# A two-block network on one core: the gate table of the expert layer built by indirect accumulating DMAs instead of one-hot products

## The reference

```python
q = (xt @ wq).reshape(T, 8, 2, 128)
s1, s2 = q[:, :, 0] @ k1.T, q[:, :, 1] @ k2.T            # (T, 8, 128) each
v1, i1 = top_k(s1, 16); v2, i2 = top_k(s2, 16)           # first choice, per half
cand = v1[..., :, None] + v2[..., None, :]               # 256 pair sums per head
sc, pos = top_k(cand, 16)                                # second choice
eidx = (i1 * 128 + i2 at pos); gate = softmax(sc)        # (T, 128) each
act = gelu(sum_d xb[t, d] * u_tab[eidx[t, k], d])
out[t] = sum_k gate[t, k] * act[t, k] * v_tab[eidx[t, k]]
```

## Time and profile before

| what | value |
|---|---|
| median of three runs | 3072.06 us |
| span of the profiled execution (the page gives no other time of it) | 3070.2 us |
| PE busy | 3026.7 us (99%) |
| DVE / ACT / POOL busy | 2206.3 / 1491.0 / 418.5 us |
| granted TensorE clock | 0.996 over the span |
| chain that ended last | PE 85%, DVE 5%, POOL 4%, issue 4% |
| DMA | 579.55 MB, 189 GB/s mean |

### The profile page before, as it was taken

One profiled execution on the slowest core, in us unless ns is written; L12 is line 12 of the kernel. 1 busy time (PEld: TensorE's weight loads), 2 busy tenths in 40 slices (PEclk: granted clock), 3 DMA queues, 4 the chain that ended last, 5 costly groups with the idle time before them and its releaser, 6 DMA issues.

```text
span 3070.2 us, 56622 instructions
## 1 busy us (share of the span) xinstructions
PE 3026.7 (99%) x19590; PEld 2701.3 (88%) x19590; DVE 2206.3 (72%) x3890; ACT 1491.0 (49%) x2330; POOL 418.5 (14%) x246
## 2 busy tenths in 40 slices
PE   8999999999999999999999999999999999999998
PEld 7889888888888888899999988888899999988887
DVE  6677566666756667669788777776659978767776
ACT  4455444444644444444455445555444454545554
POOL 0001000000011002038700000001118810000000
PEclk9999999999999999999999999999999999999999
DMA  6543255555434554457766677775447765577775
GB/s 222 187 160 119 90 169 188 168 187 187 136 98 129 187 190 135 166 183 228 217 189 182 203 241 241 240 241 181 161 158 226 227 196 183 181 247 242 240 240 187
DMA packets 213022, 579.55 MB, mean 189 GB/s; under 512 B 23744, under 2 KB 88544, under 8 KB 212368
## 3 DMA queue, kind: packets, MB, share of 16 engines
q1 hardware_dynamic: 209504, 563.67, 57.2%
q0 software_dynamic: 3376, 13.94, 1.4%
HBM read 541.34 MB, written 36.18 MB: 188 GB/s over the span
## 4 chain that ended last, share of the span: by engine, by line
PE 85%; DVE 5%; POOL 4%; issue 4%; ACT 2%; DMA 1%; SPq 0%; POOLq 0%; ACTq 0%; DVEq 0%
PE acc L745 32%; PE work L688 24%; PE work L698 9%; PE work L700 5%; POOL wsp L661 3%; PE acc L1142 3%; PE acc L807 3%; PE acc L1276 3%; DVE wsp L438 1%; ACT wsp L435 1%; PE work L1176 1%; PE work L944 1%; PE work L958 1%; PE work L1064 0%; POOL st L563 0%
## 5 line engine op out<-in xcount | busy, mean ns | idle before, releaser
L438 DVE TENSOR_TENSOR wsp<-ring,wsp 128x1024 fp32r<-128x1024 f32 x824 | 1004.4, 1227 | 489.9 <-ACT wsp L435 489.0
L435 ACT ACTIVATE wsp<-ring 128x1024 fp32r<-128x1024 f32 x944 | 984.6, 1052 | 577.4 <-PE work L688 373.8
L688 PE MATMUL work<-xsp,wsp 128*128 128x256 f32 x7872 | 982.3, 285 | 3.2 <-DVE xsp L1762 2.0
L688 PEld LDWEIGHTS work<-xsp,wsp 128*128 128x128 f32 x7872 | 955.1, 192 | 6.3 <-issue 3.0
L745 PE MATMUL acc<-wsp,hsp 128*128 128x512 f32 x4128 | 955.9, 390 | 4.7 <-DVE hsp L1850 1.9
L745 PEld LDWEIGHTS acc<-wsp,hsp 128*128 128x128 f32 x4128 | 769.5, 188 | 168.6 <-issue 4.3
L698 PE MATMUL work<-xsp,wsp 128*128 128x512 f32 x1408 | 503.3, 399 | 7.0 <-DVE xsp L1759 5.6
L700 PE MATMUL work<-xsp,wsp 128*128 128x256 f32 x1408 | 395.6, 281 | 0.0
L698 PEld LDWEIGHTS work<-xsp,wsp 128*128 128x128 f32 x1408 | 265.1, 188 | 74.9 <-DVE xsp L1759 6.6
L661 POOL TENSOR_TENSOR wsp<-ring,wsp 128x1024 fp32r<-128x1024 f32 x120 | 305.8, 2556 | 156.7 <-ACT wsp L435 156.1
L1689 ACT ACTIVATE hsp<-arena 128x256 fp32r (+1 forms) x256 | 107.1, 418 | 353.2 <-PE acc L745 341.1
(11 more groups left out here) (344 smaller groups left out, 2316.8 us busy)
## 6 DMA issues: line engine op xcount, KB each, us to landing
ring<-in_stream SPq DMA_DIRECT2D x944, 512.0 KB, 3.4
back<-acts_dram SPq DMA_DIRECT2D x252, 128.0 KB, 3.2
acts_dram<-acts SPq DMA_DIRECT2D x128, 128.0 KB, 3.6
acts_dram<-arena SPq DMA_DIRECT2D x124, 128.0 KB, 4.2
rows_sb<-in_rows POOLq DMA_DIRECT2D x10, 512.0 KB, 6.3
h_saved_dram<-h POOLq DMA_DIRECT2D x2, 1024.0 KB, 5.0
h<-h_saved_dram POOLq DMA_DIRECT2D x2, 1024.0 KB, 6.8
scratch<-in_levels POOLq DMA_DIRECT2D x3, 448.0 KB, 4.3
```

Of the source, the lines that this page charges most:

```text
L435: self.eng.activation(dst[:, 0, :], src, ACT.Copy).then_inc(high_done, 1)
L438: self.eng.tensor_tensor(dst[:, 1, :], src, dst[:, 0, :].bitcast(F32), ALU.subtract)\
L688: mm = pe.matmul(out_, lhsT=w[:, a, 128 * c:128 * c + 128], rhs=xsp[:, b, c, :], start=(c == 0 and n == 0), stop=(c == DC - 1 and n == 2))
```

## The change

1. The gates no longer pass PE. `gates_dram`, one table per layer in DRAM (4194304 floats, ordered key, expert within key, token), is cleared beforehand and then filled by POOL: for each block and each of the 128 chosen places k, one indirect DMA adds the 128 gates of column k (one per token, 4 bytes each) at the offsets that DVE computed in `spots`. The 16 DMAs of a head go out together, and the next head's wait until all of these have landed (`scattered`), since two heads of a token may have chosen the same expert. That is 16 rounds of 16 DMAs per layer.
2. Clearing: 32 DMAs per layer of 512 KB each from a tile of zeros, half of them beside the first feed-forward part of the first block's layer l, half beside the second (`clear_gates`). Each waits for the one before.
3. One-hot tiles, transposes, the one-hot products and the filler are gone. All 128 activations stay in `arena`; V's loads bring the gate table instead (`gate_back`), 128 instead of 126 loads. SP waits for the whole scatter before it issues the first of them, and the loads of V's first weight units stand behind this wait.
4. Selection starts earlier: block 0's scores are computed between the query units, and DVE makes first choices there, a low after each. POOL makes 15 lows instead of 60. DVE makes block 1's selection with a low before each piece. ACT's two exponentials stand after U's activation 17 and 57 (`EXP_AT`).

```diff
-PEER_STAGES = [("xT", 8, 0), ("tt", 16, 16), ("score", 4, 0), ("U", U_FIRST, U_FIRST), ("selT", 2, 0),
-               ("U2", NKEYS - U_FIRST, NKEYS - U_FIRST), ("V", 0, NKEYS)]
+PEER_STAGES = [("xT", 8, 0), ("tt", 16, 16), ("score", 4, 0), ("U", NKEYS, NKEYS), ("V", 0, NKEYS)]
...
+                loads(at_unit, V.u)
+                sp.wait_ge(scattered, ROUND * PH * NB * (l + 1))
+                gate_back(l, 0)
+                gate_back(l, 1)
+                for n in range(4):
+                    load(V.u + n)
+                sp.wait_ge(unit_done, V.u)
...
+            def clear_gates(l, half):
+
+                rows_of = gates_dram[l].rearrange("(r p k n) o -> r p k (n o)", r=ZEROED, p=P, n=T)
+                for r in range(ZEROED // 2 * half, ZEROED // 2 * (half + 1)):
+                    pool.dma_start(rows_of[r], back0.unsqueeze(1).broadcast_to([P, NKEYS // ZEROED, T])).then_inc(zeroed, 16)
+                    pool.wait_ge(zeroed, 16 * (ZEROED * l + r + 1))
...
-                pool.wait_ge(g_done, GROUPS * (l + 1))
+
+                for b in range(NB):
+                    pool.wait_ge(ev("sel_ready"), NB * l + b + 1)
+                    for i in range(PH):
+                        n = PH * (NB * l + b) + i
+                        if n:
+                            pool.wait_ge(scattered, ROUND * n)
+                        for k in range(TOPK * i, TOPK * i + TOPK):
+                            pool.indirect_dma_start(out=gates_dram[l], in_=selv[:, b, 2, k:k + 1], in_offset=None,
+                                                    out_offset=bass.IndirectOffsetOnAxis(spots[:, b, k:k + 1], 0),
+                                                    compute_op=ALU.add).then_inc(scattered, 16)
+                pool.wait_ge(scattered, ROUND * PH * NB * (l + 1))
...
                 for q in range(16):
-                    G.claim(pe, q)
-                    product_unit(G, q, G.bank(q)[:, 0:T], x=None if q else X)
+                    Q.claim(pe, q)
+                    product_unit(Q, q, Q.bank(q)[:, 0:T], x=None if q else X)
+                    if q >= 3 and q % 2:
+                        scores(0, (q - 3) // 2)
+                scores(0, PH - 1)
+                for i in range(PH):
+                    scores(1, i)
...
-                        for t in range(4):
-                            for m in (1, 2, 3):
-                                mm = pe.matmul(ACC[g % 4][:, 128 * t:128 * t + 128], lhsT=slot[:, 0, t // 2, :, t % 2],
-                                               rhs=slot[:, m, t // 2, :, t % 2], start=(m == 1), stop=(m == 3))
-                        mm.then_inc(g_done, 1)
...
-                busy_bank(G, 0, 11)
-                pe.wait_ge(g_moved, GROUPS * (l + 1))
...
+                activate_all(0, EXP_AT[0])
+                exponentials(0)
+                activate_all(*EXP_AT)
+                exponentials(1)
+                activate_all(EXP_AT[1], NKEYS - 1)
...
+                split.upto(Q.u + 5)
+                for i in range(PH):
+                    dve.wait_ge(ev("scored"), PH // 2 * l + i // 2 + 1)
+                    for m in range(2):
+                        first_choice(0, i, m)
+                        if split.next < U.u + 3:
+                            low_next()
...
                 split.next = U.u + 3 + POOL_LOWS
                 dve.wait_ge(low_done, split.next)
...
+                for i in range(PH // 2):
                     for m in range(2):
+                        low_next()
+                        first_choice(1, i, m)
+                    if i == 0:
+                        gates_of(0)
+                for half in range(2):
+                    low_next()
+                    pair_sums(half)
+                    for i in range(PH // 2 * half, PH // 2 * (half + 1)):
+                        low_next()
+                        second_choice(1, i, low_next if i % 2 else None)
...
+                spots_of(1)
+                less_the_first(1)
+                low_next(3)
+                gates_of(1)
```

More of the change, by code:

```diff
@@ L298, in build_program @@
         cand2 = rows[:, 1792:2048]
-        rest = rows[:, 1920:2048]
         slot_loaded = [sem(f"slot_loaded{i}") for i in range(RING)]
@@ L403, in freed @@
                 eng.wait_ge(bank_free[(self.k + c // 2) % 4], (self.k + c // 2) // 4 + 1 + c % 2)
-        def spills(slot):
-            return len([j for j in range(U_FIRST, SPILLED) if j % 4 == slot])
         class Chain:
@@ new lines, in peer, with scores @@
+                Q, S = Group(part, "tt"), Group(part, "score")
+                def scores(b, i):
+                    Q.freed(pe, 2 * i)
+                    Q.freed(pe, 2 * i + 1)
+                    if b and i % 2 == 0:
+                        S.claim(pe, i // 2)
+                    o = (S.bank(i // 2) if b else ACC[i // 2])[:, 256 * (i % 2):256 * (i % 2) + 256]
+                    for m in range(2):
+                        mm = pe.matmul(o[:, 128 * m:128 * m + 128], lhsT=qT[:, 2 * i + m, 128 * b:128 * b + 128],
+                                       rhs=pr2[:, l, Q_K1 + 128 * m:Q_K1 + 128 * m + 128], start=True, stop=True)
+                    if i % 2:
+                        mm.then_inc(job_done if b else ev("scored"), 1)
@@ L1661, in peer @@
                     G.free(act.activation(sc1[:, 512 * q:512 * q + 512], G.bank(q)[:, :], ACT.Copy), q)
-                G, U2 = Group(part, "U"), Group(part, "U2")
-                with act.Fori(0, U_FIRST // UNITS_BODY) as it:
-                    for q in range(UNITS_BODY):
-                        split.one(G.u + q + 3, it, UNITS_BODY)
-                        G.ready_unit(act, q, it * UNITS_BODY)
-                        G.free(act.activation(arena[:, bass.ds(it * (UNITS_BODY * T) + q * T, T)],
-                                              G.bank(q)[:, 0:T], ACT.Gelu), q)
@@ L1669, in peer, with activate, exponentials @@
-                split.next = G.u + U_FIRST // UNITS_BODY * UNITS_BODY + 3
-                for b in range(NB):
+                G = Group(part, "U")
+                def activate(q, it=0):
+                    split.one(G.u + q + 3, it, UNITS_BODY)
+                    G.ready_unit(act, q, it * UNITS_BODY)
+                    G.free(act.activation(arena[:, bass.ds(it * (UNITS_BODY * T) + q * T, T)], G.bank(q)[:, 0:T], ACT.Gelu), q)
+                def exponentials(b):
                     act.wait_ge(ev("smx_ready"), NB * l + b + 1)
@@ L1672, in peer, with activate_all @@
                     act.activation(selv[:, b, 2, :], selv[:, b, 2, :], ACT.Exp).then_inc(ev("smx_exp"), 1)
-                for q in range(U_FIRST // UNITS_BODY * UNITS_BODY, U_FIRST):
-                    split.upto(G.u + q + 3)
-                    G.ready_unit(act, q)
-                    G.free(act.activation(arena[:, q * T:q * T + T], G.bank(q)[:, 0:T], ACT.Gelu), q)
+                def activate_all(first, last):
+                    rounds = (last - first) // UNITS_BODY
+                    with act.Fori(0, rounds) as it:
+                        for q in range(first, first + UNITS_BODY):
+                            activate(q, it)
+                    for q in range(first + rounds * UNITS_BODY, last):
+                        activate(q)
@@ L2325, in top16 @@
                 step(dve.match_replace(tmp, vals[:, 0:8], src, LOWEST))
+                if between is not None:
+                    between()
                 step(dve.max(vals[:, 8:16], tmp))
@@ L2371, in peer, with gates_of @@
                         .then_inc(ev("smx_ready"), 1)
[L2372 to L2375 removed]
+                def gates_of(b):
+                    g3 = by_head(b)
                     dve.wait_ge(ev("smx_exp"), NB * l + b + 1)
@@ L2380, in peer @@
                         .then_inc(ev("sel_ready"), 1)
-                    dve.wait_ge(ev("sel_ready"), NB * l + b + 1)
+                split.upto(Q.u + 5)
+                for i in range(PH):
+                    dve.wait_ge(ev("scored"), PH // 2 * l + i // 2 + 1)
+                    for m in range(2):
+                        first_choice(0, i, m)
+                        if split.next < U.u + 3:
+                            low_next()
+                split.upto(U.u + 2)
+                for q in range(4):
+                    Group(part, "score").freed(dve, q)
@@ new lines, in peer @@
+                low_next()
+                places()
+                for m in range(2):
+                    low_next()
+                    look_up(1, m, low_next)
+                spots_of(1)
+                less_the_first(1)
+                low_next(3)
+                gates_of(1)
+                left = V.u + 1 - split.next
+                with dve.Fori(0, left // RING) as it:
+                    for n in range(split.next, split.next + RING):
+                        split.one(n, it, RING)
```

307 lines of the change are left out of this document (99 added, 208 removed).

## The result

The changed kernel takes 3565.23 us (median of four runs, 3564.41 to 3565.69) against 3072.07: a ratio of 1.1604, with a 95% interval of 1.1587 to 1.162. The forecast was 3017 with a range from 2990 to 3155. The mechanism is rival B's, the scatter as the bound at SP's wait before V. It puts the time 548 us over the forecast, where B had 144 for c = 1.32.

The account below looks back on a forecast made before the run. PE, busy for 99% of the span, was taken as the bound: 101.7 us off PE, less 2 x 22.5 of waits and 2 for clearing, gives 54.7 less, so 3017 us, range 2990 to 3155, with the scatter on no path.

Parts of the forecast that it names:

- rival B: SP's wait before V: the scatter is the bound and the kernel slower, 3161 with c = 1.32; chance 0.37.
- c: POOL's scatter: time of one indirect DMA issue, taken as 0.97 us, with ends 0.53 and 1.9.
- the groups' removal: PE in U: one-hot groups and transposes go, 48.4 us a layer less, U in layer 0 some 381 us.
- the wait at the query units: PE ahead of query units 6, 10 and 14: idle 3.2 us each, 10.3 us a layer with slower units behind.
- S: U's start, from which the selection and scatter times are counted; scatter to start at S + 60, end at S + 356.
- the limit of 19.6 us a round: POOL's scatter before V: longest round with which it still ends in time, 314 us over 16 rounds.
- block 1's selection between the lows: DVE beside 40 units of U: 116 us of work against PE's 115, 5.5 us of wait, between 1 and 15.
- d: End of a scatter round on POOL: the landing waited for, taken as 3 us from 2.2 to 4.2.
- R: POOL's scatter: length of one round, 16c + d, forecast 18.5 us, 10.7 with the lower bounds.
- Rival D: Block 1's stretch: POOL's issues and DVE's operations lengthen each other, 0.6 us a low, 24 us a layer: 3065; chance 0.08.
- Rival C: DVE's waits do not arise, PE keeps units in hand; only unit 58 and half the query rounds remain: 2993; chance 0.07.
- The tail: Between the scatter's end and V: gate loads, weight load, high and low, 7 us.

Follow-up runs that it names:

- psumlow: The changed kernel with DVE's low, from unit 58 to V, subtracting PSUM banks in place of the high in SBUF (lows wrong): 3467.75 us.
- noadd: The changed kernel with the scatter's indirect DMAs writing without adding, so each write replaces the last: 3480.54 us.
- rows64: The changed kernel with each indirect DMA carrying 64 of the 128 rows, half of the gates left out: 3418.47 us.
- direct: The changed kernel with direct accumulating DMAs of the same columns to fixed places in place of the indirect ones: 3029.99 us.
- noadd4: The changed kernel with indirect DMAs writing without adding and a wait for the landings behind every fourth: 3384.76 us.

## Why the prediction was wrong

Right, by its own steps, were the groups' removal (U 379.2 us, forecast 381); the wait at the query units (3.27, forecast 3.2) and ahead of unit 58 (5.12, forecast 4.1); ahead of unit 18 1.66 + 0.60, forecast 2.6; the scatter's start (S + 59.6, forecast S + 60); the limit of 19.6 us a round and the place where a late scatter is paid, in full. Without the scatter the forecast of 3017 stands against 3029.05. Of the 12 us, 9.8 are the query rounds: PEER's start to U takes 68.4 us, 15.2 more than before, where 10.3 were forecast, mostly since two units behind each wait take 7.49 us and not 6.3. Clearing cost about 6.1 in place of 2; U was 2.1 a layer shorter than forecast. The 5.5 us for block 1's selection between the lows did not come: PE runs 38 units there in 110.60 us without a wait, where 38 x 2.88 is 109.4.

Wrong was one term of the sum: c, the cost of an indirect issue, "nearer to the one with 7 rows in each of 128 partitions, 0.97". With it fell the step that rests on it, that the scatter ends by S + 356 and is on no path. The runs put three things in its place. The 0.97 holds for an indirect write that doesn't add; adding makes it 1.55. Between any two indirect issues POOL stands 0.30 us, which the direct ones in the earlier trace rows don't do. And an issue that starts just behind a low is 1.03 us longer. The other term of a round, d, was no cause: its pause is 2.2 us on average, where 3 was taken. Together a round took 577 / 16 = 36.0 us, not 18.5, nor rival B's 24.1. Rival B's chance of 0.37 was fair for what was known, its price was not: the text itself gave 1.9 as an upper end of c, which by its own sum is R = 33.4 and 3017 + 2 x 16 x 13.8 = 3459, and then let the range end at 3155. Even the price it worked out for c = 1.32, a row of its own, is 3161 and lies outside. An unknown with ends a factor of 3.6 apart, multiplied by 512, should have set the range.

Rival D asked whether POOL's issues and DVE's operations lengthen each other. They do on one side: POOL's grow by 1.03 us, DVE's low stays at 1.22, so D's price on PE was nought and that on the scatter 63 us a layer. The earlier trace rows did not carry over from a direct to an indirect issue. The rule of the Trainium skill, "SBUF — State Buffer", section "Who interferes with whom", by which a GpSimd instruction that reads SBUF contends with a DVE instruction of two SBUF inputs, agrees with 2.58 against 1.55 in the trace, and with `psumlow`. By the section "SBUF: two separate sides" of the same page of the Trainium skill the later of the two is blocked until the first is through. For POOL the trace fits: the low at 1626.72 has 1.14 us left when the issue at 1626.80 starts, and 1.03 are added. For DVE it doesn't: 49 of layer 0's 107 lows start while an issue is already under way, and none takes over 1.26 us, so here the issue does not block the low.

Rival C's own sum was a little off: with 4 us at unit 58 and half of 10.3 left of the 22.5, it saves 13.3 us a layer and ends at 2990, not 2993. Nothing hangs on it.

The tail was forecast at 7 us and took 13.5. The kernel after, SP's queue, POOL and ACT behind the wait:
```profile
1997.32 0.81 SPq L481 DMA_DIRECT2D back<-gates_dram  x2
1997.59 0.62 POOL L644 DMA_DIRECT2D h<-h_saved_dram  x1 [1.77 <-DMA gates_dram<-rows_sb,spots]
1998.18 10.51 SPq L462 DMA_DIRECT2D ring<-in_stream  x4
...
2006.02 1.06 ACT L416 ACTIVATE wsp<-ring 128x1024 fp32r<-128x1024 f32 x1 [272.44 <-DMA ring<-in_stream]
```
The gates, the ring loads, POOL's reload of `h` and its loads of `rows_sb` start at once, and the first weights are there 8.7 us after SP goes on, where the forecast had 4.4 from a single load's median. That they hold each other up is likely, but no run takes one of them away. The other 2.2 us of the difference lie behind the weights: the first activation is multiplied and split only after the first low, from 2008.25 on.

## What to carry to other kernels

Before small products are replaced by many small DMAs, multiply the number of instructions by the price of one issue and set that against the time that hides them; a factor that no row shows takes both its ends into the range. If a cover (the time under which a chain of work is hidden) has a limit per round, work out the price at the upper bound of the round too, not at the nearest row. When an engine waits on a chain that runs elsewhere, work saved on that engine while the chain runs is worth nothing, but everything that starts the chain sooner is worth its full length.

## What the runs showed of the hardware

- An indirect DMA from POOL with 128 rows of 4 bytes took 0.97 us to issue when it writes (`noadd`), 1.55 when it accumulates, 1.40 when it accumulates 64 rows (`rows64`), and 0.30 us followed each; a direct accumulating one of the same rows took 0.89, with nothing behind it (`direct`).
- Just behind the start of a DVE operation on 128x1024 with both inputs in SBUF the accumulating issue took 2.58, and beside operations with one input in PSUM 1.55 (`psumlow`); DVE's own time stayed 1.22.
- Rounds of sixteen plain indirect writes (`noadd`) brought PE from 2573 to 1099 products in 316 us, with gaps that end on its own issue; with a wait for the landing behind every fourth (`noadd4`) PE did 2559. The cause is open, and the number in flight is not shown to be it.
